# Prompt attention of a hybrid decoder step: query tiles of 128 neighbouring tokens, laid out in strips by residue modulo 4

## The chip, the core and the metric

The kernel runs on one core of a Trainium2 chip. The metric is the time on the device in microseconds; lower is better. Everything is one launch of one program, with the instruction streams of the engines written by hand: TensorE (PE) multiplies, VectorE (DVE) and ScalarE (ACT) work on what it leaves in PSUM, GpSimd (POOL) makes the low parts of weights, and SyncE (SP) issues most DMAs.

## What is computed

A two-layer decoder step for a prompt of 512 tokens and 8 samples of 8 tokens. Each layer has a gated feed-forward block (FFN), a mixer and another FFN; the mixer of the first layer is a state-space scan, that of the second is attention with a dilated sliding window. Only the attention of the prompt is changed:

```python
ATTN_PATTERNS = ((128, 1), (512, 4), (2048, 16))      # (window, dilation) of three groups of 8 heads
j = jnp.arange(win // dil + 1)
idx = offset + qi[:, None] - dil * j[None, :]          # keys of query qi
s = q_blk . k[idx] - slope * dil * j                   # masked where idx < 0
...
w = jax.nn.softmax(jnp.stack(lses), axis=0)            # the three groups merged per position
o = jnp.sum(w[..., None] * jnp.stack(outs), axis=0)
```

A query of the prompt sees, in group 0, the 129 keys up to itself; in group 1, all earlier keys of its own residue modulo 4; in group 2, all earlier keys of its own residue modulo 16. Merging the groups by their softmax denominators is the same as one softmax over the keys of all three.

## The kernel before

Activations are feature-major: 128 features on the partitions, 576 tokens (512 of the prompt, 64 of the samples) along the free dimension. Weight products split both operands into a high and a low part and run three products in a one-pass float32 form (`product`, L1441 to L1459: 48 matmuls of 288 columns). The attention itself multiplies plain float32, for which each matmul in the program leaves two records in the trace; a transpose leaves one.

The attention mixer starts with nine units (`product` with weights of `w_att`) that make q, k and v of the first head pair for the three groups, and then has four turns, one for each pair of heads (`turn(c, last)`, L1950, L1324, L2846). In turns 0 to 2 the PE interleaves nine weight products for the next pair (`ahead(0)` to `ahead(8)`) with the attention of this one, and ends with the output projection of the pair, eight blocks that DVE adds to `x` (L2110 to L2112, L2947). Turn 3 (`last`) has no products to interleave.

**Layout.** The prompt's tokens stand sorted by residue modulo 4: the normalised input is permuted as it is written (`perm`, L906 and L2146), and so is the row of norms (`rmp`, L2811). A query tile `t` of 128 columns is thus all tokens of residue `t`. For one head, its keys are all 512 of group 0 (masked to the window by the table `d0`), and the 128 of its own residue for groups 1 and 2 (tables `d12`): 768 columns.

**A query tile.** PE: `wide_scores(t)`, two matmuls of 512 columns, one for each head of the pair, with 64 rows each, into banks 4 and 5 (L1962); `narrow_scores(t)`, four of 128 columns into banks 6 and 7 (L1969). DVE: `softmax_in(e)` for each of the two heads adds slope times distance (one instruction of 512 columns, L2856, two of 128, L2860), takes the maximum over 768 (L2863) and negates it (L2864). ACT: the exponential over 768 with its sum (L1334). DVE: `normalize(e)`, a reciprocal and a product over 768 (L2868, L2869). PE: `transposes(t, 0..2)`, twelve transposes of 128x128 in three batches of four, which share bank 2 in turns 0 to 2 (L2021); ACT copies each batch out (`probs_out`, L1350, L1352). PE: `values(t)`, twelve matmuls of 128 columns, 64 columns of weights for each head (L2033). ACT and DVE take the result out as high and low part (`heads_out` L1356, `heads_low` L2904).

**Order of the PE in a turn that is not the last**: transposes of the values (L1977), scores of tile 0, the samples' scores (L2000, L1986, L1991), and then for each `t`: `ahead(2t)`, a step of the samples, `transposes(t, 0)`, `wide_scores(t+1)`, `transposes(t, 1)`, `narrow_scores(t+1)`, `transposes(t, 2)`, a wait for DVE's evacuation of `ahead(2t)`, `ahead(2t+1)`, `values(t)`. Both products write banks 0 and 1, so each waits for the evacuation of the one before (`unit_out`, L2816 to L2825, order of the units in `QKV_ORDER`). In the last turn DVE's order is `softmax_in` of two heads, `normalize` of two heads, and so on; ACT's order puts `heads_out(t)` ahead of the exponentials of tile `t+1`.

## Time and profile before

| | us |
|---|---|
| median of 3 runs (2521.60 to 2528.89) | 2524.17 |
| profiled execution, its own time | 2517.44 |
| its span, first to last instruction | 2515.6 |
| attention: nine first products | about 1735 to 1792 of the span |
| attention: turns 0, 1, 2 | 1792.5 to 2073.5 |
| attention: turn 3 | 2073.5 to 2115 |

The page gives each engine's busy time and the chain of work that ended last. The attention is some 15% of the span, so the share of busy time over the whole says little about it; the timeline and the table of stretches do. A line of the timeline has the start in the span, the duration, engine, line, operation, output and inputs with their shape (partitions x columns) and how many instructions were merged; for the PE, `64*128` is the part of the array used, 64 rows by 128 columns. The duration of one matmul contains its way through the array; what a block costs is the distance from its start to the start of the next.

### The profile page before, as it was taken

How to read it: one execution, taken by the hardware profiler on the slowest of the kernel's cores; microseconds unless marked ns; L12 is line 12 of the kernel's file. 1: busy time of each engine (PE TensorE's matmuls, PEld its weight loads, DVE VectorE, ACT ScalarE, POOL GpSimd, SP SyncE). 2: the span in 40 equal slices, each digit the busy share in tenths (PEclk: the TensorE clock that was granted, in tenths of full speed). 3: DMA queues.
4: the chain of work that ended last, by engine and by line, in shares of the span. 5: the costliest groups of instructions: out<-in, count | busy, mean ns of one | idle time of the engine just before them, and what ended most of it. 6: DMA issues, size and time to landing. Idle time of an engine off the chain costs nothing.

```text
span 2515.6 us, 48796 instructions
## 1 busy us (share of the span) xinstructions
PE 2448.1 (97%) x18955; PEld 2372.2 (94%) x18955; DVE 1892.7 (75%) x3121; ACT 1421.6 (57%) x2417; POOL 742.5 (30%) x682
## 2 busy tenths in 40 slices
PE   8999999899999998999999999999999997999998
PEld 8999999799999988999999999999998996999998
DVE  8979767878888888979776978765345448987875
ACT  7757553445555556757566757554223236766663
POOL 2222233454444542222222222223322220222223
PEclk9999999899999998999999999999999999999999
DMA  7776743123333325767655777754433423777763
GB/s 204 168 163 168 168 114 101 44 95 103 103 103 103 98 77 151 169 163 168 158 131 139 169 169 161 170 128 149 145 109 123 138 91 86 163 169 166 164 156 91
DMA packets 107137, 341.92 MB, mean 136 GB/s; under 512 B 13824, under 2 KB 17536, under 8 KB 88512
## 3 DMA queue, kind: packets, MB, share of 16 engines
q1 hardware_dynamic: 53952, 242.78, 29.0%
q0 software_dynamic: 52992, 96.49, 22.8%
q8 instruction: 131, 2.15, 0.3%
q14 instruction: 62, 0.51, 0.1%
HBM read 223.44 MB, written 19.32 MB: 96 GB/s over the span
## 4 chain that ended last, share of the span: by engine, by line
PE 85%; DVE 7%; ACT 3%; issue 3%; DMA 2%; POOL 0%; DVEq 0%; SPq 0%; ACTq 0%; POOLq 0%
PE ps L1551 14%; PE ps L1557 14%; PE ps L1549 14%; PE ps L1451 7%; PE ps L1452 7%; PE ps L1457 7%; PE ps L1566 2%; PE ps L1567 2%; DMA sb_lw<-sb_rawf 2%; PE ps L1574 2%; PE ps L1866 1%; PE ps L1867 1%; PE ps L1868 1%; PE ps L1498 1%; PE ps L1490 1%
## 5 line engine op out<-in xcount | busy, mean ns | idle before, releaser
L1551 PE MATMUL ps<-sb_ual,sb_hw 128*128 128x288 f32 x2240 | 612.2, 295 | 0.0
L1549 PE MATMUL ps<-sb_uah,sb_hw 128*128 128x288 f32 x2240 | 608.1, 294 | 0.0
L760 POOL DMA_DIRECT2D sb_lw<-sb_rawf x336 | 289.8, 864 | 961.7 <-ACT sb_lw L930 939.3
L1551 PEld LDWEIGHTS ps<-sb_ual,sb_hw 128*128 128x128 f32 x2240 | 421.2, 188 | 0.0
L1549 PEld LDWEIGHTS ps<-sb_uah,sb_hw 128*128 128x128 f32 x2240 | 420.5, 188 | 0.0
L1557 PE MATMUL ps<-sb_uah,sb_lw 128*128 128x288 f32 x2240 | 384.1, 293 | 1.6 <-DMA sb_lw<-sb_rawf 1.0
L743 POOL TENSOR_TENSOR sb_wl<-sb_raw,sb_wh 128x1024 fp32r<-128x1024 f32 (+1 forms) x106 | 260.2, 2458 | 424.7 <-ACT sb_wh L895 408.7
L1451 PE MATMUL ps<-sb_uh,sb_wh 128*128 128x288 f32 x1360 | 377.4, 304 | 5.8 <-DVE sb_zs L2578 3.2
L1452 PE MATMUL ps<-sb_ul,sb_wh 128*128 128x288 f32 x1360 | 369.4, 298 | 0.0
L1557 PEld LDWEIGHTS ps<-sb_uah,sb_lw 128*128 128x128 f32 x2240 | 328.0, 188 | 3.2 <-DMA sb_lw<-sb_rawf 1.7
L1451 PEld LDWEIGHTS ps<-sb_uh,sb_wh 128*128 128x128 f32 x1360 | 258.2, 190 | 15.7 <-issue 7.0
L929 ACT CAST sb_hw<-sb_rawf 128x512 fp32r<-128x512 f32 x336 | 207.7, 618 | 92.1 <-PE ps L1557 81.6
L1452 PEld LDWEIGHTS ps<-sb_ul,sb_wh 128*128 128x128 f32 x1360 | 258.4, 190 | 0.4
L1549 PE MATMUL ps<-sb_hh,sb_hw 128*128 128x288 f32 x896 | 244.1, 294 | 3.9 <-DVE sb_x L2331 3.9
L1551 PE MATMUL ps<-sb_hl,sb_hw 128*128 128x288 f32 x896 | 243.9, 295 | 0.0
L895 ACT CAST sb_wh<-sb_raw 128x1024 fp32r<-128x1024 f32 (+1 forms) x106 | 111.5, 1052 | 182.7 <-PE ps L1457 126.4
L930 ACT ACTIVATE sb_lw<-sb_rawf 128x512 fp32r<-128x512 f32 x336 | 211.5, 629 | 0.0
L2204 DVE TENSOR_TENSOR sb_lw<-sb_tw,sb_hw 128x1024 fp32r<-128x1024 f32 x112 | 137.2, 1225 | 95.3 <-ACT sb_hw L964 90.6
L964 ACT CAST sb_hw<-sb_tw 128x1024 fp32r<-128x1024 f32 x112 | 117.8, 1052 | 136.5 <-PE ps L1557 136.5
L1457 PE MATMUL ps<-sb_uh,sb_wl 128*128 128x288 f32 x1360 | 194.1, 295 | 0.0
L1457 PEld LDWEIGHTS ps<-sb_uh,sb_wl 128*128 128x128 f32 x1360 | 185.0, 188 | 0.0
L1549 PEld LDWEIGHTS ps<-sb_hh,sb_hw 128*128 128x128 f32 x896 | 168.1, 188 | 5.7 <-issue 5.5
(346 smaller groups left out, 5197.2 us busy)
## 6 DMA issues: line engine op xcount, KB each, us to landing
sb_lw<-sb_rawf POOLq DMA_DIRECT2D x368, 256.0 KB, 3.8
sb_rawf<-w_ffn_in SPq DMA_DIRECT2D x87, 1024.0 KB, 5.3
sb_rawf<-w_ffn_so SPq DMA_DIRECT2D x32, 1024.0 KB, 5.6
sb_raw<-w_ssd SPq DMA_DIRECT2D x64, 512.0 KB, 3.6
sb_raw<-w_att SPq DMA_DIRECT2D x40, 512.0 KB, 3.6
sb_rawf<-w_ffn_out SPq DMA_DIRECT2D x32, 384.0 KB, 3.0
sb_h<-state SPq DMA_DIRECT2D x8, 1024.0 KB, 4.9
ssm_sample<-sb_h SPq DMA_DIRECT2D x8, 1024.0 KB, 4.7
```

Source lines behind the costliest of these rows:

```text
L743: pool.tensor_tensor(wl[parity][:, 0:width], raw[:, parity, 0:width], wh[parity][:, 0:width].bitcast(F32), ALU.subtract).then_inc(wl_done, 1)
L760: pool.dma_start(slot(lw, p), rawf[:, s % 2, i * BL:(i + 1) * BL], accum_op=ALU.add).then_inc(ld_in[i], 16)
L929: nc.scalar.copy(slot(hw, p), src).then_inc(hd_done, 1)
L930: nc.scalar.activation(slot(lw, p), src, ACT.Copy, scale=-1.0).then_inc(nd_done, 1)
L964: nc.scalar.copy(slot(hw, 7, 2), tw[:, 2 * BL:4 * BL]).then_inc(ht34_done, 1)
L1451: pe.matmul(ps[:, b, 0:n], w, rh[:, k, t0:t0 + n], start=first and k == 0, stop=False)
L1452: pe.matmul(ps[:, b, 0:n], w, rl[:, k, t0:t0 + n], start=False, stop=False)
L1457: ins = pe.matmul(ps[:, b, 0:n], w, rh[:, k, t0:t0 + n], start=False, stop=last and k == nk - 1)
L1549: pe.matmul(out, w[:, k * P:(k + 1) * P], high[k], start=begins and k == 0, stop=False, skip_group_check=True)
L1551: pe.matmul(out, w[:, k * P:(k + 1) * P], low[k], start=False, stop=False, skip_group_check=True)
L1557: ins = pe.matmul(out, v[:, k * P:(k + 1) * P], high[k], start=False, stop=k == 3, skip_group_check=True)
L2204: V.tensor_tensor(slot(lw, 7, 2), tw[:, 2 * BL:4 * BL], slot(hw, 7, 2).bitcast(F32), ALU.subtract).then_inc(lt34_done, 1)
```

## The change

Queries are no longer sorted by residue. A query tile `t` is the 128 neighbouring tokens 128t to 128t+127, and within the tile the 128 rows of the score matrix are four strips of 32, one for each residue modulo 4. Group 0 then needs the keys of this tile and the one before (128 or 256 columns, `near_keys`); groups 1 and 2 need, in each strip, the keys of that residue up to this tile, 32(t+1) columns each (`far_keys`). The score row of one head has 192, 384, 448 and 512 columns for the four tiles (`KEYS`) and fits one bank.

- **Scores**: one strip of 32 output rows at a time: 8 near matmuls (4 strips, 2 heads) of 128 or 256 columns and 16 far ones of 32(t+1) columns, 24 in place of 6. The query operand has a step of 4 elements. Near and far of a head share a bank, 4 to 7 by `score_bank(t, j)`.
- **Softmax**: one instruction over `KEYS[t]` columns for the three of before; one table `dist`, with the ratio of the groups' slopes worked into it, for `d0` and `d12`; maximum, exponential and normalising over `KEYS[t]`. The probabilities `pr` have two buffers by tile.
- **Transposes**: 3 for each head in tile 0, 4 in the others (30 for 48 in a turn), into the score bank of the head, so that the batches of a tile don't wait for a shared bank; two copies by ACT for three.
- **Values**: 2 or 4 near matmuls of 128 columns and 16 far ones of 32 columns (78 for 48 in a turn), with 32(t+1) rows.
- **Order**: in turns 0 to 2, `scores(0)` and `scores(1)` stand at the start of the turn, both batches of transposes stand alone between `ahead(2t)` and `ahead(2t+1)`, and `scores(t+2)` follows `values(t)`.
- **Layout**: the permutation at the writing of `uh` and `ul` and of the norms is gone (one instruction for two, twice for each of 8 blocks; two copies less). The keys of groups 1 and 2 (`i` = 4 and 7, products 6 and 8 in `QKV_ORDER`) are written by residue at their evacuation, by three instructions for one. The values of groups 1 and 2 are read by residue at their transposes.

The core of the diff:

```diff
-                    def wide_scores(t):
-                        if t:
-                            pe.wait_ge(max_done, c * 8 + 2 * t)
+                    def scores(t):
+                        near, n = near_keys(t), far_keys(t)
+                        if t >= 2:
+                            pe.wait_ge(pt_done, c * 8 + (2 * (t - 2) + 2))
                         for j in range(2):
                             r = slice(HD * j, HD * j + HD)
-                            pe.matmul(ps[:, 4 + j, :], qkv[r, 0, rows(t)], qkv[r, 1, 0:SEQ], start=True, stop=True)
-                    def narrow_scores(t):
+                            for q in range(DIL):
+                                pe.matmul(ps[32 * q:32 * q + 32, score_bank(t, j), 0:near], of_residue(qkv[r, 0, rows(t)], q),
+                                          qkv[r, 1, (t + 1) * P - near:(t + 1) * P], start=True, stop=True)
                         for g in (1, 2):
+                            for q in range(DIL):
+                                for j in range(2):
+                                    r = slice(HD * j, HD * j + HD)
+                                    far = ps[32 * q:32 * q + 32, score_bank(t, j), near + (g - 1) * n:near + g * n]
+                                    keys = qkv[r, 3 * g + 1, q * P:q * P + n]
+                                    ins = pe.matmul(far, of_residue(qkv[r, 3 * g, rows(t)], q), keys, start=True, stop=True)
                         ins.then_inc(sc_mm, 1)
...
+                    def transposes(t, j):
+                        pe.wait_ge(norm_done, c * 8 + (2 * t + j + 1))
+                        near, n = near_keys(t), far_keys(t)
+                        for k in range(near // P):
+                            pe.transpose(ps[:, score_bank(t, j), rows(k)], pr[:, t % 2, j, rows(k)], ident[:, :])
+                        for g in (1, 2):
+                            probs = pr[:, t % 2, j, near + (g - 1) * n:near + g * n]
+                            ins = pe.transpose(ps[0:n, score_bank(t, j), rows(near // P + g - 1)], probs, ident[:, :])
+                        ins.then_inc(pt_mm, 1)
...
                         for g in (1, 2):
+                            for q in range(DIL):
+                                at = (blocks + g - 1) * P + 32 * q
+                                for j in range(2):
+                                    r = slice(HD * j, HD * j + HD)
+                                    ins = pe.matmul(ps[r, head_bank(t, last), 32 * q:32 * q + 32], vt[0:n, g, q, r],
+                                                    pt[0:n, j, at:at + 32], start=False, stop=g == 2, skip_group_check=True)
...
-                            transposes(t, 0)
-                            if t < CH - 1:
-                                wide_scores(t + 1)
-                            transposes(t, 1)
-                            if t < CH - 1:
-                                narrow_scores(t + 1)
-                            transposes(t, 2)
+                            for j in range(2):
+                                transposes(t, j)
                             pe.wait_ge(q_evac, c * 9 + (10 + 2 * t))
                             ahead(2 * t + 1)
                             sample_step(2 * t + 1)
                             values(t)
+                            if t < CH - 2:
+                                scores(t + 2)
...
+                    if i in (4, 7):
+                        cut = HALF // DIL
+                        V.tensor_tensor(residue(dst[:, 0:SEQ])[:, :, 0:cut], by_residue(ps[:, b, 0:HALF]),
+                                        by_residue(rms[:, 0:HALF]), ALU.mult)
+                        V.tensor_tensor(residue(dst[:, 0:SEQ])[:, :, cut:P], by_residue(ps[:, b + 1, 0:SEQ - HALF]),
+                                        by_residue(rms[:, HALF:SEQ]), ALU.mult)
+                        ins = V.tensor_tensor(dst[:, SEQ:TOK], ps[:, b + 1, SEQ - HALF:HALF], rms[:, SEQ:TOK], ALU.mult)
...
-                        V.scalar_tensor_tensor(pr[:, j, 0:SEQ], d0[:, t, :], slp[:, one(c * 2 + j)], ps[:, 4 + j, :],
-                                               ALU.mult, ALU.add)
-                        for g in (1, 2):
-                            o = slice(SEQ + (g - 1) * P, SEQ + g * P)
-                            ins = V.scalar_tensor_tensor(pr[:, j, o], d12[:, g - 1, :], slp[:, one(c * 2 + (AH * g + j))],
-                                                         ps[:, 6 + j, rows(g - 1)], ALU.mult, ALU.add)
-                        step(ins)
-                        step(V.reduce_max(nmx[:, e:e + 1], pr[:, j, :], AX.X))
+                        p = pr[:, t % 2, j, 0:KEYS[t]]
+                        step(V.scalar_tensor_tensor(p, dist[:, sum(KEYS[:t]):sum(KEYS[:t + 1])], slp[:, one(c * 2 + j)],
+                                                    ps[:, score_bank(t, j), 0:KEYS[t]], ALU.mult, ALU.add))
+                        step(V.reduce_max(nmx[:, e:e + 1], p, AX.X))
```

## Rows read from the trace of the kernel before

**Rows 1.** The page: busy time of each engine, and the chain by engine.
```profile
PE 2448.1 (97%) x18955; PEld 2372.2 (94%) x18955; DVE 1892.7 (75%) x3121; ACT 1421.6 (57%) x2417; POOL 742.5 (30%) x682
...
PE 85%; DVE 7%; ACT 3%; issue 3%; DMA 2%; POOL 0%; DVEq 0%; SPq 0%; ACTq 0%; POOLq 0%
```

**Rows 2.** Busy time by stretch, turns 1 and 3; columns in the first row.
```profile
core 0: us, PE busy (x) PEld busy (x) DVE busy (x) ACT busy (x) POOL busy (x), PEclk, DMA share, GB/s
...
1886.50:1980.10 93.60, 92.81 (x822) 84.72 (x820) 45.73 (x110) 30.63 (x57) 24.04 (x10) 1.00 0.36 121
...
2073.50:2115.00 41.50, 29.36 (x342) 22.31 (x341) 32.34 (x92) 20.37 (x47) 0.00 (x0) 0.96 0.21 73
```

**Rows 3.** Timeline of the PE, start of turn 0: scores of tile 0.
```profile
1794.17 1.13 PE L1962 MATMUL ps<-sb_qkv 64*128 64x512 f32 x4
1795.13 0.61 PE L1969 MATMUL ps<-sb_qkv 64*128 64x128 f32 x8
1795.67 0.52 PE L2000 MATMUL ps<-sb_ident,sb_qkv 128*64 128x128 f32 x3
```

**Rows 4.** Timeline of the PE, turn 0: transposes of tile 0 with scores of tile 1.
```profile
1805.93 0.60 PE L2021 MATMUL ps<-sb_ident,sb_pr 128*128 128x128 f32 x4
1806.46 1.13 PE L1962 MATMUL ps<-sb_qkv 64*128 64x512 f32 x4
...
1808.86 0.66 PE L2021 MATMUL ps<-sb_ident,sb_pr 128*128 128x128 f32 x4
1809.27 0.38 PE L1451 MATMUL ps<-sb_uh,sb_wh 128*128 128x288 f32 x1
```

**Rows 5.** Chain in order of time (start, us, what): values of tile 0, transposes of tile 3.
```profile
1815.90 1.46 PE ps L2033 x24
...
1863.41 1.31 PE ps L2021 x12
```

**Rows 6.** Timeline of the PE: matmuls in narrow parts of the array, and what followed.
```profile
486.50 0.45 PE L1749 MATMUL ps<-sb_sgs,sb_xds 64*64 64x64 f32 x8
486.88 0.33 PE L1754 MATMUL ps<-sb_ident,sb_ysc 128*128 128x128 f32 x1
...
1843.38 1.95 PE L2059 MATMUL ps<-sb_vc,sb_pts 128*32 128x128 f32 x64
1845.27 0.33 PE L2021 MATMUL ps<-sb_ident,sb_pr 128*128 128x128 f32 x1
```

**Rows 7.** Timeline of DVE in the last turn: softmax of one head, one normalising.
```profile
2076.71 0.75 DVE L2856 SCALAR_TENSOR_TENSOR sb_pr<-sb_d,sb_slp,ps 128x512 f32<-128x512 f32 x1
2077.37 0.60 DVE L2860 SCALAR_TENSOR_TENSOR sb_pr<-sb_d,sb_slp,ps 128x128 f32<-128x128 f32 x2
2078.01 0.95 DVE L2863 TENSOR_REDUCE sb_nmx<-sb_pr 128x1 f32<-128x768 f32 x1
...
2079.07 0.74 DVE L2856 SCALAR_TENSOR_TENSOR sb_pr<-sb_d,sb_slp,ps 128x512 f32<-128x512 f32 x1
...
2082.17 0.62 DVE L2869 TENSOR_SCALAR sb_pr<-sb_pr,sb_rcp 128x768 f32<-128x768 f32 x1
```

**Rows 8.** Timeline: instructions with and without permutation, the PE's wait for one, an evacuation.
```profile
1713.42 1.22 ACT L907 ACTIVATE sb_uh<-sb_x,sb_gains 128x512 fp32r<-128x512 f32 x1 [1.47 <-DVE sb_x L2474]
1714.79 0.67 ACT L914 ACTIVATE sb_sqx<-sb_x 128x576 f32<-128x576 f32 x1
1714.92 1.34 DVE L2148 SCALAR_TENSOR_TENSOR sb_ul<-sb_x,sb_gains,sb_uh 128x512 fp32r<-128x512 f32 x2 [1.53 <-ACT sb_uh L908]
...
1733.26 0.40 PE L1451 MATMUL ps<-sb_uh,sb_wh 128*128 128x288 f32 x1 [0.48 <-DVE sb_ul L2148]
...
1863.52 0.76 DVE L2824 TENSOR_TENSOR sb_qkv<-ps,sb_sqx 128x576 f32<-128x576 f32 x1 [5.78 <-PE ps L1457]
```

**Rows 9.** Timeline, last turn: values of tile 2, exponential of tile 3, first output block.
```profile
2105.86 1.53 PE L2033 MATMUL ps<-sb_pt,sb_vt 128*64 128x128 f32 x24
...
2107.62 0.92 ACT L1334 ACTIVATE sb_pr<-sb_pr,sb_nmx 128x768 f32<-128x768 f32 x1
...
2114.79 0.37 PE L2110 MATMUL ps<-sb_oh,sb_wh 128*128 128x288 f32 x1 [0.99 <-DVE sb_ol L2904]
```

More of the change, by code:

```diff
@@ L53 @@
 KEYC = 512
+KEYS = (192, 384, 448, 512)
 KEYR = ((0, 128), (128, 256), (384, 128))
@@ L2030, in values @@
+                        for k in range(blocks):
                             for j in range(2):
                                 r = slice(HD * j, HD * j + HD)
[L2032 to L2033 removed]
+                                pe.matmul(ps[r, head_bank(t, last), 0:P], vt[:, 0, t + 1 - blocks + k, r], pt[:, j, rows(k)],
+                                          start=k == 0, stop=False, skip_group_check=True)
```

176 lines of the change are left out of this document (77 added, 99 removed).

## The prediction

> **What bounds the kernel now.** The page comes first: the PE is busy for 97% of the span and makes 85% of the chain that ended last [rows 1]. That is an average over FFNs, scan and attention, and the change touches the attention alone, so I read next the table of stretches [rows 2]. In turn 1, as in turns 0 and 2, the PE is busy 92.8 of 93.6 us while DVE has 45.7 and ACT 30.6: a microsecond of PE work removed there is a microsecond won, and a microsecond of softmax removed is worth nothing. In turn 3 the PE is busy only 29.4 of 41.5 us and DVE 32.3: there is no weight product under which the softmax could hide, and DVE with the hand-overs between engines sets the pace. So the change has to be costed twice: in turns 0 to 2 by PE time, in turn 3 by the length of a dependent chain.
>
> **PE time in turns 0 to 2, before.** I take distances from start to start. Scores of one tile standing alone: 0.96 wide and 0.54 narrow, 1.50 us [rows 3]. Transposes of a tile woven with the scores of the next: from 1805.93 to 1809.27, 3.34 us, three times a turn [rows 4]; that is more than 1.31 for twelve transposes in a row plus 1.50 [rows 5], because the batches share a bank and the array's layout changes four times. Tile 3 has its transposes alone, 1.31, and values cost 1.46 a tile [rows 5]. Sum for a turn: 1.50 + 3 x 3.34 + 1.31 + 4 x 1.46 = 18.7 us.
>
> **After, transposes.** 30 at 1.31 / 12 = 0.109 us [rows 5] make 3.3 us. But between `ahead(2t)` and `ahead(2t+1)` now only these stand, and the second product must wait for DVE's evacuation of the first. That evacuation ran from 1863.52 for 0.76 us, to 0.87 us after the product's end at 1863.41 [rows 5, 8]; before, 1.31 or 3.34 us of PE work covered it. Now tile 0 has 6 x 0.109 = 0.65 us: 0.25 us of waiting. Tiles 1 and 2 have a step of the samples as well and stay covered. Tile 3 has 0.87 us, and its evacuation is that of `ahead(6)`, keys of group 1, which becomes three instructions with a step of 4 in both inputs. Such an instruction isn't in the trace on PSUM; the nearest are two permuted ones of 576 columns together, 1.34 us, where the plain form takes 0.76 or so [rows 8]. So 0.9 to 1.5 us; I take 1.2, by its middle, since the step costs DVE something in the one row there is: 0.5 us of waiting (0.1 to 0.8). Transposes with waits: 4.0 us (3.6 to 4.6).
>
> **After, scores.** 24 matmuls a tile in strips of 32 output rows and halves of 64 input rows. Strips run side by side: 32 matmuls of 128 columns (64 records) took 1845.27 - 1843.38 = 1.89 us over four strips, 0.059 each or 0.236 in each strip [rows 6]. Halves run side by side too: the two wide matmuls have 4 x 128 columns each and took 0.96 together, where one after the other at the strip's rate would be 1.89 [rows 3, 6]. If strips and halves both run at once (eight parts), a tile is bound by its columns: near 0.47 (0.24 in tile 0) and far 0.12, 0.24, 0.35, 0.47, together 2.8 us a turn. If no matmul is ever handed to the array faster than 0.059, the fastest that a row shows, a tile takes 24 x 0.059 = 1.42, 5.7 a turn. If the halves take turns as well, near 0.94 and far 0.94, 7.1 a turn. The eight parts together are in no row; I take 1.2 us a tile, 4.8 a turn, nearer to the rate shown than to the columns, because the far matmuls are so short that something other than their columns must bind.
>
> The PE's rate of hand-over is where a rule speaks against this change. The Trainium skill (TensorEngine Tiling, Instruction Overhead) says each matmul carries about 60 cycles of overhead, so that a factor should not be taken from a dimension that is already small, and another page (TensorE: Matmul & The Clock Gate, "Wait — 56ns, not 53.3ns?") gives about 62 ns per MATMUL where firmware decodes. By the second, read for each matmul of the program, a tile's scores would take 24 x 0.062 = 1.5 us, 6.0 a turn in place of 4.8; the row's 0.059 agrees with it as well as with the column bound, so it can't tell them apart. Read for each record it would be 3.0 a tile, which the row contradicts (1.89 / 64 = 0.030).
>
> **After, values.** Near: 14 matmuls at 1.46 / 12 = 0.122 [rows 5], 1.7 us. Far: 64 of 32 columns with 64 columns of weights. From below, a quarter of 0.122 by columns: 2.0. From above, four matmuls of 64 columns with 64 columns of weights took 0.38, entering and leaving included, 0.095 each [rows 6]: 6.1. I take the 0.059 of the strips with something for the changes of layout (32 and 64 rows in tiles 0 and 1), 4.3. Values: 6.0 us (3.7 to 7.8), no gain against 5.8.
>
> **After, the rest of a turn.** `ahead(8)` is evacuated by residue too, and DVE's eight additions to `x` queue behind it while the PE waits for the banks: 0.4 us (0.2 to 0.7). Reading queries and values with a step of 4 as weights is in no row; I cost it at nothing, since weights are loaded under the running matmuls, and count up to 0.3 us a turn for it. The softmax of a tile now has its scores waiting and half the columns: it stays under a product. Sum: 4.0 + 4.8 + 6.0 + 0.4 = 15.2 against 18.7: 3.5 us a turn, **10 us in three turns**. With all the low bounds it would be 8.4 a turn, with all the high ones a loss of 1.5.
>
> **Turn 3.** DVE takes 2079.07 - 2076.71 = 2.36 us to bring one head's scores to a maximum: 1.30 for three instructions of 768 columns, then 0.95 for the maximum and the negation [rows 7]. A single instruction takes 0.64 / 2 = 0.32 at 128 columns and 0.66 at 512, so 0.38, 0.55, 0.60, 0.66 for the four widths; the maximum shrinks by some 1.2 ns a column, the normalising (0.62 for 768) by some 0.7. For the six heads of tiles 0 to 2 that is 4.7 + 3.1 + 1.8 = 9.6 us of DVE, all ahead of the values of tile 2. I don't take it whole: the samples' scores and maximum stay as they are, the PE does `scores(1)` ahead of them, and ACT's exponentials wait for `heads_out`. From the values of tile 2 to the first output block there are 8.9 us [rows 9]: ACT copies the heads out, then starts the exponentials of tile 3. That part shrinks by 256 of 768 columns in two exponentials and two normalisings and by four transposes, 1 to 1.3 us. I expect values of tile 2 some 8 us earlier, the output block **9 us earlier** (5 to 12).
>
> **Opening.** The PE waited 0.48 us for the permuted `ul` of the last block [rows 8]. ACT's 1.22 us and 0.34 more become one plain pass like the 0.67 us square, DVE's 1.34 becomes 0.8: the wait goes, but next is the evacuation of the last first unit (`i` = 7), 0.2 to 0.6 us longer and on the path. Net gain 0.3 us (-0.5 to 1). The two copies of norms go free, the table is smaller, and both had slack of several us.
>
> **Sum.** 10 + 9 + 0.3 = 19.3, call it 19. The profiled execution would go from 2517.4 to 2498; the median of the runs is 6.7 us above that execution, so 2524.2 - 19 = **2505 us**. Own range of this case: 2497 to 2512.
>
> **Rivals.**
> *Hand-over binds the PE.* At 7.1 for scores and 6 to 7.8 for values a turn of kind 0 to 2 wins nothing or 1 us, and only turn 3 gains, 5 to 9 us: 2512 to 2519. For it: 102 tiny matmuls a turn are added and the fastest rate in the trace is that of the strips; against it: that rate is what columns alone would give.
> *Columns bind.* Eight parts run at once and short matmuls are as cheap as their columns: 6 us a turn and 11 in turn 3, 29 us: 2495.
> *Short matmuls don't overlap (slower).* If each of the 128 far matmuls of a turn costs what a full transpose does and more, because a change of strip, half or number of rows drains the array, the gain is gone: 19 us over four turns is 4.8 us, 0.037 for each over my 0.07, so it decides at 0.107 each. At 0.14 each, 128 x 0.07 x 4 = 36 us more: 2541, at 0.12 each 2530. For it: the woven block of rows 4 costs 0.5 us more than its parts. Against it: rows 6, where four strips and two halves overlap.
> *It does not do what it says.* The softmax's saving is real only in turn 3; if the samples' chain and not DVE sets that turn, it gives 4 us. With a PE gain of 10 that is 2510, inside the range.
>
> **Chances.** Forecast 0.60; hand-over binds 0.19; columns bind 0.13; short matmuls don't overlap 0.08. The range of 8 in 10 takes in most of both neighbours: 2491 to 2518. What a measurement can tell from no change is about 0.3%, 7.6 us, so faster means below 2516.6: 0.60 + 0.13 and half of 0.19, 0.83; within 0.3% 0.10; slower 0.07.
>
> **What would show it.** In turns 0 to 2, a period of about 90.1 us in place of 93.6. Scores of a tile from start to the next line: 1.2 us (0.7 if columns bind, 1.42 or more if hand-over does). Far values of a tile near 1.0 us. A wait of the PE on DVE's evacuation after the transposes of tiles 0 and 3, 0.25 and 0.5 us. Turn 3 from 41.5 to 32 us, DVE's head of tile 1 at about 1.4 us for 2.36. The prediction is wrong if far matmuls cost over 0.1 us each, if DVE or ACT become late in turns 0 to 2, or if the PE's clock, 0.96 in turn 3 [rows 2], falls further as the PE has less to do there.

## The result, and the profile after

| | before | after |
|---|---|---|
| median of the runs | 2523.41 us (2521.6 to 2528.89) | 2506.44 us (2505.85 to 2507.19) |
| ratio | 1 | 0.9929, 95% interval 0.9912 to 0.9946 |
| profiled execution: own time, span | 2517.44, 2515.6 us | 2507.19, 2505.3 us |
| a turn of kind 0 to 2 | 93.6 us | 89.7 us |
| turn 3, to its first output block | 41.2 us | 34.0 us |

The change makes the kernel 17 us faster; 2505 had been predicted. The profiled execution of before is one of its short ones, so the two spans show only 10.3 us of the 17. The table of the attention's pieces is the better comparison, since it leaves out what did not change. Each number is a distance between two starts of the PE in the two traces; the line at 1693 is the same product of FFN2 in both.

| piece | before | after | difference |
|---|---|---|---|
| start to the product at 1693 us of before (unchanged code) | 1693.0 | 1698.8 | +5.8 |
| from there to the start of turn 0 (the opening) | 99.7 | 97.3 | -2.5 |
| turns 0 to 2 | 280.9 | 269.2 | -11.7 |
| turn 3 to its first output block | 41.2 | 34.0 | -7.2 |
| last output projection | 11.4 | 12.3 | +0.9 |
| FFN3 and the end (unchanged code) | 389.4 | 393.7 | +4.3 |

The attention is 20.4 us shorter in this pair, and the unchanged code 10.1 us longer. How much of the 10.1 is chance is one of the questions below.

The page of after, busy time and the chain by engine, answers [rows 1]: the PE has 12 us less and a smaller share of the chain, in spite of 744 matmul records more.

```profile
PE 2436.4 (97%) x19699; PEld 2372.8 (95%) x19699; DVE 1862.7 (74%) x3063; ACT 1394.9 (56%) x2393; POOL 740.2 (30%) x682
...
PE 84%; DVE 6%; DMA 3%; ACT 3%; issue 2%; POOL 0%; DVEq 0%; SPq 0%; ACTq 0%; POOLq 0%
```

Busy time by stretch in after, turn 1 and turn 3, with the columns in the first row, as in [rows 2]:

```profile
core 0: us, PE busy (x) PEld busy (x) DVE busy (x) ACT busy (x) POOL busy (x), PEclk, DMA share, GB/s
1885.90:1975.60 89.70, 87.74 (x1007) 83.30 (x1006) 40.03 (x99) 24.99 (x53) 24.00 (x10) 1.00 0.37 127
2065.30:2099.30 34.00, 28.04 (x526) 22.69 (x525) 22.37 (x76) 15.57 (x43) 0.00 (x0) 0.81 0.25 90
```

Turn 1 reads as before, the PE filling it (87.7 of 89.7 us), with 2 us of idle time that were 0.8. In turn 3 DVE has lost 10 of its 32.3 us, and the granted clock is 0.81 where it was 0.96: the turn is shorter but the PE is slower in it.

The PE in turn 1, from values of tile 0 to scores of tile 2 (start, duration, line, tiles, count; a bracket is idle time before it):

```profile
1906.91 0.44 PE L2040 MATMUL ps<-sb_pt,sb_vt 128*64 128x128 f32 x4
1907.28 1.12 PE L2047 MATMUL ps<-sb_pt,sb_vt 32*64 32x32 f32 x32
1908.33 0.69 PE L1972 MATMUL ps<-sb_qkv 64*32 64x256 f32 x16
1908.81 0.68 PE L1980 MATMUL ps<-sb_qkv 64*32 64x96 f32 x32
1909.42 0.40 PE L1459 MATMUL ps<-sb_uh,sb_wh 128*128 128x288 f32 x1
```

The scores of a tile, start to start, are 1909.42 - 1908.33 = 1.09 us, where a tile standing alone had 1.50 [rows 3]. That holds 48 records for 24 matmuls, 0.023 us a record: less than the 0.030 of the fastest row of before [rows 6]. The far values, 16 matmuls in 32 records, are 1908.33 - 1907.28 = 1.05 us, 0.066 each.

The transposes of tiles 0 and 3 in turn 1, with what the PE waits for behind them, and DVE's evacuation of `ahead(6)`, keys of group 1, in three parts:

```profile
1899.28 0.27 PE L2023 MATMUL ps<-sb_ident,sb_pr 128*128 128x128 f32 x1
...
1900.37 0.40 PE L1459 MATMUL ps<-sb_uh,sb_wh 128*128 128x288 f32 x1 [0.27 <-DVE sb_qkv L2832]
...
1951.64 0.38 PE L2023 MATMUL ps<-sb_ident,sb_pr 128*128 128x128 f32 x2
...
1953.25 0.40 PE L1459 MATMUL ps<-sb_uh,sb_wh 128*128 128x288 f32 x1 [0.57 <-DVE sb_qkv L2828]
```
```profile
1951.91 0.68 DVE L2824 TENSOR_TENSOR sb_qkv<-ps,sb_rms 128x288 f32<-128x288 f32 x1 [5.83 <-PE ps L1465]
1952.51 0.55 DVE L2826 TENSOR_TENSOR sb_qkv<-ps,sb_rms 128x224 f32<-128x224 f32 x1
1952.97 0.22 DVE L2828 TENSOR_TENSOR sb_qkv<-ps,sb_rms 128x64 f32<-128x64 f32 x1
```

Tile 0 takes 1.09 us and tile 3 1.61 us from its first transpose to the next product. Both waits of the prediction are there, and the three parts take 1953.11 - 1951.91 = 1.20 us from start to the next instruction, against 0.76 for the one of before [rows 8].

Turn 3: DVE's head of tile 1, and the PE from values of tile 2 to the first output block, the stretch of [rows 7, 9]:

```profile
2074.36 0.60 DVE L2865 SCALAR_TENSOR_TENSOR sb_pr<-sb_dist,sb_slp,ps 128x384 f32<-128x384 f32 x1
2074.99 0.55 DVE L2867 TENSOR_REDUCE sb_nmx<-sb_pr 128x1 f32<-128x384 f32 x1
...
2075.65 0.60 DVE L2865 SCALAR_TENSOR_TENSOR sb_pr<-sb_dist,sb_slp,ps 128x384 f32<-128x384 f32 x1
```
```profile
2089.59 0.66 PE L2040 MATMUL ps<-sb_pt,sb_vt 128*64 128x128 f32 x8
...
2095.55 1.12 PE L2040 MATMUL ps<-sb_pt,sb_vt 128*64 128x128 f32 x8 [0.67 <-ACT sb_pt L1360]
2096.45 1.87 PE L2047 MATMUL ps<-sb_pt,sb_vt 128*64 128x32 f32 x32
2099.31 0.58 PE L2119 MATMUL ps<-sb_oh,sb_wh 128*128 128x288 f32 x1 [0.99 <-DVE sb_ol L2909]
```

DVE's head is 1.29 us for 2.36. The values of tile 2 come 24.3 us into the turn, for 32.3. But from there to the output block it now takes 9.72 us, for 8.93: the last tile's far values take 1.87 us, where such a block takes 1.12 in turn 1. The table of stretches of 5 us says why: PEclk is 0.50, the lower level of 1.2 GHz, in two of them.

```profile
2080.30:2085.30 5.00, 5.00 (x90) 3.76 (x89) 3.08 (x10) 2.13 (x8) 0.00 (x0) 0.50 0.01 3
2085.30:2090.30 5.00, 5.00 (x99) 4.44 (x96) 3.33 (x8) 1.92 (x6) 0.00 (x0) 0.91 0.01 3
2090.30:2095.30 5.00, 3.04 (x39) 2.37 (x35) 2.05 (x7) 2.96 (x9) 0.00 (x0) 0.77 0.59 193
2095.30:2100.30 5.00, 3.76 (x44) 3.66 (x45) 0.38 (x1) 0.58 (x2) 0.00 (x0) 0.50 0.04 16
```

The reading of the pair leaves three theories to be tried. **First**: turns 0 to 2 are PE time alone, made of hand-over, evacuation waits and columns as the prediction has them. **Second**: turn 3 fell short because of the clock, not because of the softmax. **Third**: what the unchanged code lost is chance, against its rival that work behind the attention gives a part of the gain back.

### The profile page after: what moved, and what is told of

Its sections match the earlier page's. It is cut to its first block, busy times and chain, and to the rows that moved or that the text cites. A ratio compares the mean times of both kernels' runs of the same rounds, so it can differ in the third digit from the quotient of the medians.

```text
span 2505.3 us, 50171 instructions
## 1 busy us (share of the span) xinstructions
PE 2436.4 (97%) x19699; PEld 2372.8 (95%) x19699; DVE 1862.7 (74%) x3063; ACT 1394.9 (56%) x2393; POOL 740.2 (30%) x682
## 4 chain that ended last, share of the span: by engine, by line
PE 84%; DVE 6%; DMA 3%; ACT 3%; issue 2%; POOL 0%; DVEq 0%; SPq 0%; ACTq 0%; POOLq 0%
PE ps L1559 14%; PE ps L1565 14%; PE ps L1557 14%; PE ps L1459 7%; PE ps L1460 7%; PE ps L1465 7%; DMA sb_lw<-sb_rawf 3%; PE ps L1574 2%; PE ps L1575 2%; PE ps L1582 2%; PE ps L1874 1%; PE ps L1875 1%; PE ps L1876 1%; PE ps L1506 1%; PE ps L1498 1%
```

## Experiments

All are the changed kernel with one edit (the last two sections combine several), and each was compared with the kernel before on the same chip. The experiments ran on three chips, with medians of 2524.2 (again to far_values_twice), 2526.7 (plain_keys to warm_order) and 2522.3 us (wide_far to best2) for the kernel before, so whole times are compared by their ratios. The table has the pieces of every profile, measured as above (turn = mean of turns 0 to 2; "one" is a single timed execution, without an interval), and the mean granted clock over turn 3. The names are again (the changed kernel once more), max_twice (every row maximum twice), wide_far, wide_values and narrow_values (far scores and far values with other widths), plain_keys (keys evacuated in one instruction), order (another order of the weight units), warm (turn 3 filled), warm_order (both) and best2 (samples' scores moved as well).

| kernel | time, us | ratio to before | opening | turn | turn 3 | PEclk in turn 3 | last projection | FFN3 and end |
|---|---|---|---|---|---|---|---|---|
| before | | 1 | 99.7 | 93.6 | 41.2 | 0.96 | 11.4 | 389.4 |
| after | 2506.4 | 0.9929 | 97.3 | 89.7 | 34.0 | 0.81 | 12.3 | 393.7 |
| again | 2506.0 | 0.9931 (0.9911 to 0.9951) | 97.3 | 89.7 | 34.0 | 0.81 | 12.3 | 391.9 |
| max_twice | 2505.9 | 0.9941 (0.9920 to 0.9963) | 97.2 | 89.7 | 32.4 | 0.95 | 11.4 | 391.4 |
| far_scores_twice | 2514.5 | 0.9960 (0.9942 to 0.9978) | 97.2 | 92.7 | 35.6 | 0.89 | 12.3 | 391.4 |
| far_values_twice | 2516.3 | 0.9971 (0.9961 to 0.9981) | 97.3 | 93.6 | 35.7 | 0.86 | 11.3 | 391.6 |
| plain_keys | 2497.8 | 0.9888 (0.9871 to 0.9905) | 96.8 | 88.8 | 31.1 | 0.94 | 12.2 | 390.9 |
| order | 2501.5 | 0.9897 (0.9875 to 0.9920) | 96.7 | 88.8 | 34.0 | 0.81 | 12.3 | 392.0 |
| warm | 2503.2 | 0.9917 (0.9895 to 0.9940) | 97.2 | 89.7 | 32.0 | 1.00 | 11.3 | 391.8 |
| warm_order | 2497.7 | 0.9892 (0.9874 to 0.9910) | 96.8 | 88.8 | 32.0 | 1.00 | 11.3 | 391.4 |
| wide_far | 2502.1 (one) | | 97.2 | 90.0 | 30.1 | 1.00 | 11.3 | 392.3 |
| wide_values | 2503.1 (one) | | 97.3 | 89.9 | 30.7 | 0.94 | 11.4 | 392.5 |
| narrow_values | 2499.9 (one) | | 97.2 | 88.2 | 31.0 | 0.86 | 12.3 | 393.2 |
| best2 | 2497.2 | 0.9902 (0.9886 to 0.9919) | 98.2 | 87.4 | 31.1 | 1.00 | 11.4 | 393.6 |

The turn's period is the sharpest measure here: between the turns of a profile, and between after and again, it repeats within 0.2 us (with one exception, told below), while whole times scatter by 6 us and more.

### The changed kernel once more

> The changed kernel once more, with nothing altered, for what two executions of one program differ by. In the first pair of profiles the work from the first output block of turn 3 to the end of the span took 400.8 us before (2515.6 less 2114.79) and 406.0 after (2505.3 less 2099.31), although no line of it was changed; and the stretch up to 1693 us ran 5.8 us later in the changed kernel. Theory C (chance): these stretches differ from execution to execution, so this run shows 400 to 403 us behind the output block, and the time is within 3 us of 2506. Theory S (the gain is given back, since work behind the attention now starts before what it needs is there): 404.5 to 407 again. The turn period of turns 0 to 2 is 89.7 us within 0.2 in both, turn 3 34.0 within 0.5.

The attention repeats to 0.2 us in each piece, so the periods above can be trusted to that. Behind the output block there are 404.1 us, on the border of the two theories. The other profiles settle part of it. The stretch up to 1693 us, where no line was changed, is 1695.7 to 1700.9 in the thirteen profiles of the changed kernel and its variants and 1693.0 in the one of before. FFN3 and the end take 390.9 to 393.7 in the thirteen, 389.4 in the one. The one profile of before is thus short where no change can have reached it, as its own time, 6 us below its median, says too. Chance is the likely reading, but one profile of before can't show it. The medians differ by 17 to 18 us, the attention's pieces, projection included, by 20.4: some 2 to 3 us are left that may be a true give-back in FFN3. The PE's waits for `lw` of FFN3 (1.7 us in after, 0.9 in this run, none among the largest of before) point to it. That isn't shown either.

### Every row maximum twice

```
 step(V.reduce_max(nmx[:, e:e + 1], p, AX.X))
+step(V.reduce_max(nmx[:, e:e + 1], p, AX.X))
```

> Every row maximum of the prompt's softmax is taken twice on VectorE (0.35, 0.55, 0.62 and 0.69 us by tile, two of each, 4.4 us a turn, some 5 with the gap behind each). Theory of the prediction (TensorE alone sets turns 0 to 2, the softmax sets turn 3): period of turns 0 to 2 unchanged at 89.7, within 0.3; turn 3 longer by 2 to 5, 3.5 expected; in all +3.5 us, 2510. Rival (the narrower softmax is what shortened turns 0 to 2 as well): +4.4 us in each turn, +17 to +20 in all, 2524.

Turns 0 to 2 did not move by 0.1 us, with 4.4 us more of DVE in each: the narrower softmax is worth nothing there, as the stretches said. Turn 3 got **shorter**, 32.4 for 34.0 us, with more work in it. No part of the prediction gives that. The stretches of this kernel's turn 3:

```profile
2080.90:2085.90 5.00, 5.00 (x98) 3.91 (x96) 4.76 (x12) 2.85 (x9) 0.00 (x0) 0.78 0.01 3
2085.90:2090.90 5.00, 4.58 (x89) 3.74 (x90) 4.56 (x10) 2.33 (x8) 0.00 (x0) 1.00 0.01 3
2090.90:2095.90 5.00, 2.74 (x47) 2.04 (x45) 2.96 (x10) 3.15 (x9) 0.00 (x0) 1.00 0.53 170
2095.90:2100.90 5.00, 3.95 (x57) 3.64 (x58) 1.84 (x3) 1.08 (x3) 0.00 (x0) 1.00 0.09 39
```

Apart from its first row the clock is at 1.00, where it was at 0.50 to 0.91. The PE's longest wait grew as the added work would have it (2.6 us in place of 1.3 ahead of the transposes of tile 1), and the low stretch came out shorter. That the added maxima brought this about isn't shown: the clock of turn 3 differs as much between kernels whose DVE does the same work in it (see the turn filled with spare matmuls). Compared at the same clock, the added work does cost time: wide_values, below, has 0.94 in turn 3 for the 0.95 here and takes 30.7 us, plain_keys has 0.94 and takes 31.1, so 32.4 is 1.3 to 1.7 us more. This is less than the 2 to 5 expected, and a comparison with after alone, at 0.81, hides it.

### Far score matmuls twice

```
-ins = pe.matmul(far, of_residue(qkv[r, 3 * g, rows(t)], q), keys, start=True, stop=True)
+for _ in range(2):
+    ins = pe.matmul(far, of_residue(qkv[r, 3 * g, rows(t)], q), keys, start=True, stop=True)
```

> Each of the 16 far score matmuls of a tile is issued twice in a row with the same output, so 64 more matmuls a turn, 128 records. The profile of the changed kernel has 2.21 us for the 128 far records of a turn, and that hardly by their width (0.42 to 0.52 us for 32 records at widths of 32, 64, 96 and 128). Theory H (a short matmul costs its place in the stream, about 17 ns a record, with eight parts of the array open): +2.2 us a turn, +6.6 in turns 0 to 2 and, beside the softmax, +0 to +2 in turn 3: 2513. Rival O (the records overlap with what stands beside them, and a repeat of a matmul in the same part must wait until that part has ended, 64 keys at four cycles of 2.4 GHz 0.11 us, 128 keys 0.21): +0.11 x 64 = 7 us a turn, +21 and more, 2527 or above.

Turn 1 went from 89.6 (the run above) to 92.3: 2.6 to 2.7 us for 64 matmuls, 0.042 each or 0.021 a record. In turn 2 it was 3.5, and the mean of three turns 3.0; the 0.8 us more stand in one place there, in the scores at the head of the turn, with an idle stretch of 0.5 us to which the view gives no releaser. Theory H had 2.2. It is far from the rival's 7, but the mean hides a slope. By tile, the blocks of scores grew by 1.06 us for the 32 repeats with 32 and 64 keys (0.033 each), by 0.69 for the 16 with 96 keys (0.043) and by 2.00 - 1.14 = 0.86 for the 16 with 128 keys (0.054):

```profile
1930.17 0.69 PE L1972 MATMUL ps<-sb_qkv 64*32 64x256 f32 x16
1930.66 1.58 PE L1981 MATMUL ps<-sb_qkv 64*32 64x128 f32 x64
1932.17 0.40 PE L1459 MATMUL ps<-sb_uh,sb_wh 128*128 128x288 f32 x1
```

So where two matmuls in a row go to the same part of the array the columns do show, though the repeat with 128 keys costs only a quarter of the rival's 0.21 us.

### Far value matmuls twice

```
-ins = pe.matmul(ps[r, head_bank(t, last), 32 * q:32 * q + 32], vt[0:n, g, q, r],
-                pt[0:n, j, at:at + 32], start=False, stop=g == 2, skip_group_check=True)
+for again in range(2):
+    ins = pe.matmul(ps[r, head_bank(t, last), 32 * q:32 * q + 32], vt[0:n, g, q, r],
+                    pt[0:n, j, at:at + 32], start=False, stop=g == 2 and again == 1, skip_group_check=True)
```

> Each of the 16 far value matmuls of a tile is issued twice in a row, so these groups' values count twice (the output is another). 64 more matmuls a turn. The changed kernel takes 0.064 us for each of them (4.11 us for 64), far above its 32 columns (at four cycles 0.053 us, for half of the array's columns). Theory H (the price is that of a place in the stream): +4.1 us a turn, +12.3 in turns 0 to 2, and +4 to +6 in turn 3, whose end waits for TensorE at half clock: 2523. Rival (the price is the wait for the transposed probabilities and for the other half of the array, so a repeat is nearly free): +1 us a turn, 2510.

+3.9 us a turn, 0.061 each, against +4.1 expected. Turn 3 grew by 1.7 and not by the 4 to 6 expected. With 1.0 us less in the projection the pieces sum to 11.7 + 1.7 - 1.0 = 12.4, though the medians differ by 10 only. That is the scatter of whole times again, and why the periods are used here. One far value costs half as much again as one far score, 0.061 against 0.042, though the score has up to four times the columns. The next three look at why.

### Wide far scores

```
-far = ps[32 * q:32 * q + 32, score_bank(t, j), near + (g - 1) * n:near + g * n]
-keys = qkv[r, 3 * g + 1, q * P:q * P + n]
+f0 = near + (g - 1) * n
+far = ps[32 * q:32 * q + 32, score_bank(t, j), f0:f0 + P]
+keys = qkv[r, 3 * g + 1, q * P:q * P + P]
```

> Every far score matmul is 128 keys wide in all tiles, not 32, 64, 96 and 128; the 16 a tile stay 16, and the columns too many are overwritten by the next group's or not read, so the output is unchanged. 3072 columns a turn are added. Theory H (the price of a short one is its place in the stream, with eight parts of the array at work at once): 3072 columns over eight parts at 1.67 ns (four cycles of 2.4 GHz) are 0.64 us at the most, and less as far as they lie below the hand-over; period 89.7 to 90.2. Rival (the columns of one row half follow one another, so four parts are at work at once): +1.3 us a turn, 91.0. Rival with no overlap: +5.1 us, 94.8.

+0.3 us a turn for 3072 columns. Less than the 0.64 that eight parts at once would take for them (0.71 at the 0.236 / 128 = 0.00184 us a column of [rows 6]), far less than 1.3 or 5.1. So eight parts do run at once, and most of the columns added lie below the price of the hand-over.

### Far values of 64 columns

```
-ins = pe.matmul(ps[r, head_bank(t, last), 32 * q:32 * q + 32], vt[0:n, g, q, r],
-                pt[0:n, j, at:at + 32], start=False, stop=g == 2, skip_group_check=True)
+b = 32 if q == 3 else 0
+ins = pe.matmul(ps[r, head_bank(t, last), 32 * q - b:32 * q - b + 64], vt[0:n, g, q, r],
+                pt[0:n, j, at - b:at - b + 64], start=False, stop=g == 2, skip_group_check=True)
```

> Every far value matmul moves 64 columns of probabilities, not 32 (two strips' worth, so the output is another); weights and number of matmuls are the same. It costs 0.061 to 0.064 us now. Theory H (the place in the stream sets it, and the two halves of the array's columns work at the same time): 64 columns at four cycles are 0.107 us in each half, 0.053 for each matmul of two that overlap, below 0.061, so the period stays at 89.7 within 0.3. Rival C (the halves do not overlap, and 32 columns at 0.053 us plus a little are what 0.061 is): 0.107 to 0.115 each, +2.9 to +3.4 us a turn, 92.6 to 93.1.

89.9, +0.2 us: twice the columns in all 64 matmuls cost nothing to speak of. Rival C falls. The timeline has the same block as above with 64 for 32 columns, 1909.52 - 1908.44 = 1.08 us for 1.05:

```profile
1908.44 1.15 PE L2048 MATMUL ps<-sb_pt,sb_vt 32*64 32x64 f32 x32
1909.52 0.69 PE L1972 MATMUL ps<-sb_qkv 64*32 64x256 f32 x16
```

### Far values with 32 columns of weights

```
+r = slice(HD * j, HD * j + 32)
 ins = pe.matmul(ps[r, head_bank(t, last), 32 * q:32 * q + 32], vt[0:n, g, q, r],
```

> Every far value matmul makes only 32 of a head's 64 features, so its weight tile is 32 columns wide, not 64, as in the scores; half of the far groups' output is left out (the output is another). Number of matmuls and moving columns are unchanged. A repeated far score matmul (32 weight columns) cost 0.041 us, a repeated far value matmul (64) 0.061. Theory W (the load of the weights, 32 or 64 columns for each of the two records of a float32 matmul, sets the distance between them): 0.041 each, -1.3 us a turn in turns 0 to 2, period 88.4. Rival (it is the 32 moving columns or the accumulation in place): unchanged, 89.7 within 0.2.

The same block, 32 records again, with half the weights:

```profile
1906.56 0.69 PE L2048 MATMUL ps<-sb_pt,sb_vt 32*32 32x32 f32 x32
1907.18 0.69 PE L1972 MATMUL ps<-sb_qkv 64*32 64x256 f32 x16
```

1907.18 - 1906.56 = 0.62 us for 16 matmuls, 0.039 each, where 64 columns of weights take 0.066. The period fell by 1.5 us, 0.023 for each of the 64. That is what a far score costs, which has 32 columns of weights as well. So the price of a short float32 matmul here goes with the width of its weight tile and, up to 64, not with the columns that move. That the loads themselves queue is one reading. With 32 columns of weights a matmul also writes half the output partitions and takes a smaller part of the array, and no run separates these three; the runs show the dependence, not its inside.

### Keys evacuated in one instruction

```
-if i in (4, 7):
+if i in ():
```

> The evacuation of keys 1 and 2 (units i = 4 and 7) is again one instruction over all 576 columns instead of three, so the keys of the dilated groups lie in token order and the output is another; nothing else is changed. The three parts take 0.68, 0.55 and 0.22 us in the changed kernel, 1.45 in all, the one instruction 0.76. Theory of the prediction (an evacuation costs where TensorE waits for it: before transposes of tile 3 and at the head of the turn, and nowhere else): these two waits shrink by 0.5 to 0.7 each, the period of turns 0 to 2 from 89.7 to 88.5, the wait at the head of turn 0 from 1.34 to 0.85; -4 us in all, 2502. Rival (something else is late there, VectorE's evacuation is not what TensorE waits for): periods stay at 89.7.

Period 88.8, 0.9 us less. The waits of the PE in turn 1, in after and then in this run (what waits for what, total, times, longest):

```profile
PE ps L1459 <- DVE sb_qkv L2828: 0.6, 1, 0.6
PE ps L2000 <- ACT sb_vts L1351: 0.6, 1, 0.6
PE ps L2119 <- DVE sb_x L2952: 0.5, 1, 0.5
PE ps L1459 <- DVE sb_qkv L2832: 0.3, 1, 0.3
```

```profile
PE ps L2000 <- ACT sb_vts L1351: 0.6, 1, 0.6
PE ps L1459 <- DVE sb_qkv L2832: 0.3, 1, 0.3
```

The wait for the third part of the evacuation (L2828, tile 3) is gone, and so is the output projection's wait for DVE's additions (L2952), which queued behind the other long evacuation. This is the gain of the theory, a little under its 1.2. The profiled turn 3 took 31.1 us here, though the edit touches nothing in it. Its clock was 1.00 in the first stretch where after has 0.50, and fell only later, for a shorter time. So the whole time fell by more than the 4 us expected, and what turn 3 has of it is the clock's:

```profile
2077.60:2082.60 5.00, 4.91 (x101) 3.74 (x97) 4.56 (x12) 3.62 (x12) 0.00 (x0) 1.00 0.01 3
2082.60:2087.60 5.00, 3.77 (x107) 3.28 (x105) 2.29 (x7) 1.71 (x5) 0.00 (x0) 1.00 0.13 21
2087.60:2092.60 5.00, 3.97 (x48) 3.48 (x48) 1.66 (x6) 1.71 (x6) 0.00 (x0) 0.72 0.52 192
2092.60:2097.60 5.00, 4.01 (x22) 3.74 (x18) 1.83 (x4) 1.66 (x3) 0.00 (x0) 0.59 0.01 3
```

### Another order of the weight units

```
-QKV_ORDER = (2, 5, 8, 0, 1, 3, 4, 6, 7)
+QKV_ORDER = (2, 5, 8, 0, 1, 4, 3, 7, 6)
```

> The units of the weights are taken in the order (2, 5, 8, 0, 1, 4, 3, 7, 6) in place of (2, 5, 8, 0, 1, 3, 4, 6, 7), so that keys 1 and 2 come at positions 5 and 7, whose evacuations have values(t) beside them (1.49 us of TensorE's work against 1.45 of evacuation), and queries at 6 and 8, which nothing covers. Theory of the cover: the same gain as with the plain evacuation, period 88.5, -4 us in all, 2502, output unchanged. Rival (1.49 does not cover 1.45 plus the hand-over to VectorE, some 0.1 to 0.2 us at positions 5 and 7): 88.8, -3 us. Second rival (no gain, because the wait only moves): 89.7.

88.8 again, equal to the plain evacuation within 0.1, with the keys by residue. The three parts are as long as ever (0.68, 0.55 and 0.22 at 1960.04 in this kernel) but values of a tile stand beside them. So the cost of the residue layout was its place in the order, not its work. At tile 3 the view has no wait left between the transposes and the next product, 1953.34 - 1952.24 = 1.10 us for 1.61, and at the opening the wait is 0.85 for 1.34:

```profile
1952.24 0.38 PE L2023 MATMUL ps<-sb_ident,sb_pr 128*128 128x128 f32 x2
...
1953.34 0.40 PE L1459 MATMUL ps<-sb_uh,sb_wh 128*128 128x288 f32 x1
```

### Turn 3 filled with spare matmuls

```
+def fill(n):
+    for _ in range(n):
+        pe.matmul(ps[:, 2, 0:P], ident[:, :], ident[:, :], start=True, stop=True)
 if last:
+    pe.wait_ge(own_done, c + 1)
     for t in range(CH):
+        fill(0 if t == 0 else 5)
         for j in range(2):
             transposes(t, j)
         sample_step((0, 2, 4, 0)[t])
+        fill(3)
         values(t)
...
+if last:
+    fill(4)
 pe.wait_ge(sol_done, c + 1)
 pe.wait_ge(ol_done, c * 4 + 4)
```

> Turn 3 gets matmuls of the identity by itself (128 by 128, 0.21 us each at full clock) into a free bank where TensorE waits in it: five before the transposes of tiles 1 to 3, three before each tile's values, four before the output projection. Theory K (the tail of turn 3 is long because the granted clock falls to 0.5 after TensorE's waits: 0.50 in 2080 to 2085 and 2095 to 2100 us, against one such stretch of some 3 us before): clock near 1.0 throughout, turn 3 to its first output block from 34.0 to 31.5, the work behind it shorter by 1 to 2; -4 us in all, 2502. Rival D (the softmax sets turn 3, whatever the clock): turn 3 stays at 34 within 0.5 or grows by the filling, 2506 to 2508. The run with the doubled maxima speaks for K: it had 4.4 us more of VectorE in turn 3, its clock read 0.78 to 1.0, and its turn 3 took 32.4.

The granted clock is 1.00 in every stretch of the turn; the two that answer to the two low ones of after:

```profile
2076.90:2081.90 5.00, 5.00 (x109) 4.43 (x109) 3.98 (x11) 2.43 (x10) 0.00 (x0) 1.00 0.00 0
...
2091.90:2096.90 5.00, 4.95 (x62) 4.59 (x59) 2.26 (x4) 1.56 (x3) 0.00 (x0) 1.00 0.02 7
```

Turn 3 took 32.0 for 34.0 us and the projection behind it 11.3 for 12.3: 3.0 us in all in the pieces. The whole times don't show it: the intervals of the ratio, here and for again, overlap. Theory K holds, with two limits. The filling itself costs: with full clock and no filling turn 3 took 30.1 us (wide_far), so of the 3.9 us by which that is below 34.0 the filling takes 1.9 back. And the low clock isn't bound to the schedule. The five unfilled kernels after, again, order, wide_values and wide_far differ in turn 3 by 0.3 us of PE work at most, yet their clock in it reads 0.81 three times, 0.94 and 1.00, and the turn takes 34.0, 34.0, 34.0, 30.7 and 30.1 us. A mean of 0.81 is half clock for some 13 of 34 us, by the two levels of 1.00 and 0.50. Two executions of one program differ as well: over the whole span the four of again have 0.987, 0.990, 0.988 and 0.988. All three filled profiles have 1.00. So filling buys certainty more than time.

### Order and filling together

> Both the new order of the units and the filling in turn 3. If the two effects are independent, as one lies in turns 0 to 2 and the other in turn 3 and behind it, the gains add: -4 and -4, 2498, ratio to the kernel before 0.990. If the clock in turn 3 or the waits behind the turns eat a part: 2500 to 2503.

The two edits add up in the pieces: period 88.8, turn 3 32.0, projection 11.3. 2497.7 us, ratio 0.9892 (0.9874 to 0.9910), with an upper end just below the lower end of the changed kernel's (0.9911).

### With the samples' scores moved

```
 scores(1)
...
-sample_scores()
+if last:
+    sample_scores()
...
 for j in range(2):
     transposes(t, j)
+if t == 0:
+    sample_scores()
```

Beside this, `ahead(0)` waits for `vt_done` of groups 0 and 1, DVE does `sample_own` and `sample_max` behind the evacuation of `ahead(0)`, and the filling is `fill(3)`, `fill(2)`, `fill(4)`.

> The new order of the units and the filling of turn 3 (three matmuls of the identity before the transposes of tiles 1 to 3, two before the values, four before the output projection), and in turns 0 to 2 the samples' scores moved from the head of the turn to behind transposes(0), where TensorE waits some 0.4 us for the evacuation of ahead(0); the 0.6 us wait at the head for the samples' turned values goes with it. New is a wait of ahead(0) for two of ScalarE's value evacuations (2 x 0.67 us beside 1.66 of scores). On VectorE sample_own and sample_max (some 3 us) move behind the evacuation of ahead(0), ahead of the softmax of tile 1. Expected if both waits were TensorE's alone: period 88.77 to 87.8, turn 3 to its first output block 31.5, -3.5 us against the variant with order and filling (2497.7), so 2494, ratio 0.9875. Rival (the moved VectorE work delays tile 1's softmax or heads_low and a wait comes up there, or the waits return at ahead(0)): period 88.8 or above, 2497 to 2499.

The period is 87.4, 1.4 us less again, better than the 87.8 expected, and the view of waits has no row left for the PE in turn 1. It is busy 87.31 of 87.5 us:

```profile
1884.60:1972.10 87.50, 87.31 (x1008) 83.40 (x1007) 39.54 (x99) 24.99 (x53) 24.01 (x10) 1.00 0.39 130
```

Turn 3 is 31.1, with 21 spare matmuls for the 31 of warm. The opening is 98.2 us, 1.4 more than in the other kernels with this order: the PE's clock reads 0.83 from 1743 to 1753 us, as it does in before and in none of the others. The attention from the opening to the projection is 403.0 us, against 406.4 with order and filling and 412.8 in the changed kernel. But the ratio to before is 0.9902, no less than the 0.9892 of warm_order. In its profile the unchanged code up to 1693 us took 3.1 us more than in that of warm_order and FFN3 2.2 us more, which together are more than the 3.4 won, and of the size by which such stretches scatter here. The gain in the attention is shown, one in the whole time isn't.

## Why the prediction was right, point by point

**What bounds the turns.** Right: turns 0 to 2 are PE time, and DVE's work there is free. The doubled maxima moved nothing.

**Turns 0 to 2.** 90.1 us predicted, 89.7 measured. In turn 1 by its terms: transposes with their waits 1.09 + 0.79 + 0.85 + 1.61 = 4.3 us (4.0 predicted); scores 3.9 (4.8 predicted, 2.8 by columns and 5.7 by hand-over); values 6.0 (6.0). The term that was mis-sized is the scores. The prediction stayed near the 0.059 us a matmul of [rows 6], as the fastest that a row shows; with eight parts open it is 0.035 in tiles 0 and 1 (1.66 us for 48), 0.045 and 0.048 in tiles 2 and 3. [rows 6] had four strips with 128 columns each and was bound by columns, as the prediction itself said against the rival. The values were right by luck in part: 0.059 "with something for the changes of layout" came to 0.064, but it goes with the 64 columns of weights (0.039 with 32), and the strips of [rows 6], from which the 0.059 came, had 32.

**The rule of the skill.** By the 62 ns per MATMUL that the Trainium skill (TensorE: Matmul & The Clock Gate, "Wait — 56ns, not 53.3ns?") gives for decoding by firmware, a tile's scores would be 1.5 us, an estimate. They are 1.09 for 24 matmuls, and a repeated one costs 0.042, so that price is not paid here. Whether this program's matmuls are decoded by firmware no run shows, so the figure itself is not refuted. The direction of the other rule of the Trainium skill (TensorEngine Tiling, Instruction Overhead) holds: 3072 more columns cost 0.3 us a turn and 64 more far matmuls 2.7 to 3.9, so at these sizes the count is paid far more than the columns.

**Evacuation by residue.** 1.2 us predicted, 1.20 from start to the next instruction. Waits 0.25 and 0.5 predicted, 0.27 and 0.57 measured. `ahead(8)`, 0.4 us: the two sites together give 0.9 in the run with plain keys, as 0.5 and 0.4.

**Opening.** 0.3 us predicted (-0.5 to 1), 2.5 measured; nine of the profiles lie at 97.2 to 97.3 us. The edge costs were as foreseen, but the prediction did not look at the clock there. Before, PEclk was 0.83 in the 10 us behind the PE's 1.8 us wait for `wh`; after, with the same wait, it is 1.00. The rows, before and then after:

```profile
1740.00:1750.00 10.00, 10.00 (x66) 10.00 (x65) 7.40 (x5) 1.62 (x2) 7.59 (x6) 0.83 0.62 207
```
```profile
1745.80:1755.80 10.00, 10.00 (x77) 10.00 (x77) 1.79 (x3) 1.05 (x1) 6.58 (x5) 1.00 0.75 240
```

17% of 10 us are 1.7 us, and two waits of 0.5 us (for `ul` and for `x`) are gone as well. The two waits can be put down to the permutations, though no run undid these alone. The 1.7 us can't: the low stretch came back in best2, which has no permutations either, and cost its opening 1.4 us. Of the thirteen profiles without permutations one has that stretch, and so has the only profile with them, so whether it is there may be luck. The gain without it is 0.8 to 1.1 us, at the upper bound of the prediction.

**Turn 3.** 32 us predicted, 34.0 measured. The chain was right: DVE's head is 1.29 us for the 1.4 predicted. The values of tile 2 come 8.0 us earlier in the turn for the 8 predicted, but that is luck in part, as a low stretch of the clock lies ahead of them too: in wide_far, at full clock, they come 2088.64 - 2066.49 = 22.2 us into the turn, 10.2 earlier. What failed is the last step, that the part from the values of tile 2 to the output block shrinks by 1 to 1.3 us: it grew by 0.8, since the PE ran at half clock there. In wide_far it takes 2096.60 - 2088.64 = 8.0 us for 8.9, so at full clock that step nearly holds, and the turn takes 30.1, less than predicted. The prediction named the clock as what could make it wrong, and gave it no price; it should have been a term of up to 4 us.

**The sum.** Predicted 10 + 9 + 0.3 = 19 us; in the pieces 11.7 + 7.2 + 2.5, less 0.9 in the projection, 20.4 before rounding; in the medians 17 to 18. So the total is as close as it is because too little in turns and opening, too much in turn 3 and perhaps 2 to 3 us given back in FFN3 offset each other: the number is luck in part. The working was sound in turns 0 to 2; in turn 3 it had the chain right and left the clock out.

**The rivals.** Hand-over binds: its kind of cost is real, its size for the scores too high by nearly a half (5.7 against 3.9). Columns bind: near for the scores (3.9 against 2.8), not for the values. Short matmuls don't overlap: out; the far values, at 0.064, lie well below the 0.107 from which it would have decided, the far scores further still.

## What to carry to other kernels

When work is cut into many small matmuls in parts of the array, price each by its weight tile and its place in the stream, and let the moving side grow until the columns show; price them from a row with as many parts open as the new code will have. When an evacuation gets longer, ask first whether it can trade places with one that has cover: the three instructions cost 0.9 us a turn more than one in one order, and nothing more in another. Where the PE gets less to do in a stage with waits, look at its granted clock in that stage, before and after, and give it a term of its own in the sum. And when a run gets faster with more work in it, compare it with a run at the same clock before giving the work the credit.

## What was not expected of the hardware

- A float32 matmul with 64 by 32 of the array, eight parts taken in turn, costs nearly the same whether it moves 32 or 128 columns: 3072 columns more in 64 matmuls are 0.3 us. Repeated at once in its own part it is 0.033 us with 32 and 64 columns, 0.043 with 96 and 0.054 with 128. With 64 columns of weights it is 0.061 to 0.066, and the same for 32 and 64 moving columns; with 32 columns of weights in place of these 64, 0.039.
- With 4.4 us more of DVE work turn 3 was 1.6 us shorter, as its clock happened to be higher (0.95 for 0.81); at equal clock it is 1.3 to 1.7 us longer.
- Nearly the same turn 3 took 34.0 us in three profiles, 31.1 and 30.7 in two and 30.1 in another, with the clock at 0.81, 0.94 and 1.00. In after, plain_keys and wide_far the PE's wait ahead of the transposes of tile 1 was the same, 1.3 us; the clock fell 2 us after its end in the first, 15 us after it in the second and not at all in the third. So whether it falls is not settled by the schedule alone.
